# A fused FFN and mixer layer in two-part fp32: gate and up pieces moved in between the first modulation units, x's root from token rows, filler matmuls at the norms

## What is computed

```python
mod_ctx = (silu(c_ctx)[None] @ w_ada[l] + b_ada[l]).reshape(1, N_MOD, D_MODEL)
h = adaln_in(x, g[0], sh(0), sh(1))                 # rmsnorm(x, g) * (1 + scale) + shift
x = x + 0.5 * sh(2) * rmsnorm(swiglu(h, p['w_gate'][0], p['w_up'][0], p['w_down'][0]), g[1])
h = adaln_in(x, g[2], sh(3), sh(4))
mix, new_ml, new_ssm = hybrid_mixer(h, p, ml_state, ssm_state, n_seg)
x = x + sh(5) * rmsnorm(mix, g[3])
h = adaln_in(x, g[4], sh(6), sh(7))
x = x + 0.5 * sh(8) * rmsnorm(swiglu(h, p['w_gate'][1], p['w_up'][1], p['w_down'][1]), g[5])
```

## Time and profile before

| | |
|---|---|
| median of 3 runs | 3184.39 us (3184.34 to 3184.51) |
| the profiled execution: its own time, its span | 3184.13 us, 3182.3 us |
| granted clock of PE, mean over the span | 0.981 of 2.4 GHz |
| busy share PE / PEld / DVE / ACT / POOL | 96% / 91% / 42% / 31% / 57% |
| read from memory | 519 MB, 51% of the DMA engines' time |

### The profile page before, as it was taken

How to read it: one execution, slowest core, us unless ns; L and a number is a source line. 1 busy time by engine, 2 the same in 40 slices (tenths; PEclk the granted TensorE clock), 3 DMA queues, 4 the chain that set the end, 5 groups by cost and what they waited for, 6 DMA issues and landing times.

```text
span 3182.3 us, 48743 instructions
## 1 busy us (share of the span) xinstructions
PE 3067.9 (96%) x17651; PEld 2888.2 (91%) x17651; DVE 1350.7 (42%) x3013; ACT 973.4 (31%) x1206; POOL 1829.4 (57%) x903
## 2 busy tenths in 40 slices
PE   6799999999999999899999999899999999999998
PEld 2499999999999999689999999699999999999997
DVE  0336665665656655585754353413442211100114
ACT  2232222222232223533432333432222222222221
POOL 2366556655565555546775445565655666566663
PEclk8799999999999999899999999899999999999999
DMA  9967556656666555345444544145545654444442
GB/s 335 299 205 233 194 192 201 222 191 207 196 206 220 191 195 191 120 138 156 140 132 129 120 112 164 54 139 172 178 140 162 161 144 124 129 127 128 125 125 92
DMA packets 519202, 532.22 MB, mean 167 GB/s; under 512 B 29275, under 2 KB 493635, under 8 KB 518211
## 3 DMA queue, kind: packets, MB, share of 16 engines
q1 hardware_dynamic: 483136, 509.67, 51.0%
q10 hardware_dynamic: 35971, 21.27, 2.5%
HBM read 519.12 MB, written 9.66 MB: 166 GB/s over the span
## 4 chain that ended last, share of the span: by engine, by line
POOL 39%; issue 28%; PE 25%; DVE 4%; DMA 2%; ACT 2%; POOLq 1%; ACTq 0%; DVEq 0%
POOL w_lo L2272 36%; PE banks L699 7%; PE banks L701 7%; PE banks L700 7%; POOL hid_lo L2292 1%; PE banks L759 1%; DMA AM<-in_w_in_dram 1%; DMA w_raw<-in_w_ada_dram 1%; DVE HB L1989 1%; PE banks L725 1%; PE banks L1015 0%; PE banks L1100 0%; PE banks L1120 0%; ACT AM L1214 0%; DVE banks L1571 0%
## 5 line engine op out<-in xcount | busy, mean ns | idle before, releaser
L2272 POOL TENSOR_TENSOR w_lo<-w_raw,w_hi 128x1024 fp32r<-128x1024 f32 x668 | 1599.4, 2400 | 1088.6 <-ACT w_hi L1195 1088.0
L699 PE MATMUL banks<-xn_hi,w_hi 128*128 128x384 f32 x3936 | 1342.9, 341 | 29.4 <-DVE xn_lo L1588 18.4
L701 PE MATMUL banks<-xn_hi,w_lo 128*128 128x384 f32 x3936 | 1321.8, 336 | 0.0
L700 PE MATMUL banks<-xn_lo,w_hi 128*128 128x384 f32 x3936 | 1321.8, 336 | 0.0
L1195 ACT ACTIVATE w_hi<-w_raw 128x1024 fp32r<-128x1024 f32 x668 | 706.6, 1061 | 1531.1 <-PE banks L701 714.8
L699 PEld LDWEIGHTS banks<-xn_hi,w_hi 128*128 128x128 f32 x3936 | 743.9, 189 | 51.8 <-issue 37.6
L700 PEld LDWEIGHTS banks<-xn_lo,w_hi 128*128 128x128 f32 x3936 | 743.9, 189 | 3.9 <-issue 2.9
L701 PEld LDWEIGHTS banks<-xn_hi,w_lo 128*128 128x128 f32 x3936 | 743.4, 189 | 0.0
L1657 DVE SCALAR_TENSOR_TENSOR banks<-w_raw,cT,banks 128x256 f32<-128x256 f32 x1372 | 550.6, 484 | 0.3
L1735 DVE TENSOR_TENSOR AM<-AM,banks 128x384 f32<-128x384 f32 x88 | 44.8, 551 | 622.8 <-PE banks L701 622.8
L699 PE MATMUL banks<-hid_hi,w_hi 128*128 128x384 f32 x704 | 238.0, 338 | 3.1 <-POOL hid_lo L2292 3.1
(11 more groups left out here) (251 smaller groups left out, 1812.9 us busy)
## 6 DMA issues: line engine op xcount, KB each, us to landing
w_raw<-in_w_ada_dram SPq DMA_DIRECT2D x288, 512.0 KB, 5.2
w_raw<-in_ffn_w_gate_dram SPq DMA_DIRECT2D x176, 512.0 KB, 3.8
w_raw<-in_ffn_w_up_dram SPq DMA_DIRECT2D x176, 512.0 KB, 3.7
w_raw<-in_ffn_w_down_dram SPq DMA_DIRECT2D x176, 512.0 KB, 3.7
w_raw<-in_w_in_dram SPq DMA_DIRECT2D x104, 512.0 KB, 3.7
w_raw<-in_w_out_dram SPq DMA_DIRECT2D x32, 512.0 KB, 3.5
HB<-row_wait ACTq DMA_DIRECT2D x12, 512.0 KB, 4.7
x_wait<-xT ACTq DMA_DIRECT2D x1, 3072.0 KB, 9.6
```

The source lines that it names most:

```text
L699: pe.matmul(out, wh, hi, start=start, stop=False)
L700: pe.matmul(out, wh, lo, start=False, stop=False)
L701: return pe.matmul(out, w_lo[:, w, off:off + P], hi, start=False, stop=stop)
L2272: pool.tensor_tensor(w_lo[:, slot(p), :], w_raw[:, p % NR, :], w_hi[:, slot(p), :].bitcast(F32), ALU.subtract).then_inc(w_lo_ready, 1)
```

## The change

1. The start gets 9 main pieces: quarters 0, 1, 2 of g and u of the first 256 hidden columns and of g of the second 256. Each is loaded behind the four a pieces of its unit v (`START_LOAD`) and multiplied between the third and fourth a piece of unit v + 1 (`START_MAIN`). The second g is summed in banks 4 and 5 (`gate_bank`). `START_PAIRS` sets the units at which the normed pairs are made. The first part of FFN 1 keeps 7 main pieces with the same 20 a and 4 b pieces. The loop and all later orders stay.
2. x is loaded first, all 16 transposes follow piece by piece, and x's mean square comes from DVE on token rows (`x_root`): bn_stats, a root of 128 x 3, a diagonal spread by one matmul over bank 5 and copied to SBUF. The squares, POOL's adds and the 384-wide root and inverse of x go.
3. Columns of a unit are made after the second a piece of the next one where no main piece comes before.
4. y is zeroed during unit 14 (FFN 1), and by quarters within g of the second 256 columns (FFN 2); DVE waits for it after the first part.
5. At y1 and y2 PE makes 20, at x1 and x2 34 extra products of 128 x 128 ones into bank 1 (`stay_awake`). A root on one column before each FFN tail loads ACT's table early (`warm`).
6. The fourth main piece behind x1 and x2 is split after 12 of the 16 normed tiles.

```diff
-LEAD_BODY = 2 * "aaam" + 6 * "aam" + 2 * SPREAD_END
+LEAD_BODY = "aaaaaamaaaamaaaaaaaaaaam" + SPREAD_END
-        main = [(kind, 0, q) for q in range(U) for kind in "gu"] + main[-2 * U:]
+        main = [(kind, 0, q) for q in range(0 if n else U - 1, U) for kind in "gu"] + main[-2 * U if n else -U - 1:]
-START_PIECES = ada_units(ADA_FIRST)
+START_LOAD = {5: ("g", 0, 0), 6: ("u", 0, 0), 7: ("g", 1, 0), 8: ("g", 0, 1), 9: ("u", 0, 1), 10: ("g", 1, 1),
+              12: ("g", 0, 2), 13: ("u", 0, 2), 14: ("g", 1, 2)}
+START_MAIN = {(v + 1, 2): piece for v, piece in START_LOAD.items()}
+START_PAIRS = {4: 0, 5: 1, 6: 2, 8: 3, 10: 4, 12: 5, 14: 6}
+WAKE_Y, WAKE_X = 20, 34
+ROOT_TILE = 10
+        def gate_bank(n, part, s):
+            return 4 if n == 0 and part == "first" and s else 0
# SP
+                sp.dma_start(x_tok[:, 0, :], A["x_prompt"][0]).then_inc(x_loaded, 16)
+                sp.dma_start(x_tok[:, 1:3, :], A["x_sample"][0].rearrange("(c p) n -> p c n", p=P)).then_inc(x_loaded, 16)
+                for p, (kind, v, q) in enumerate(START_PIECES):
+                    if p == 3:
+                        sp.wait_ge(x_loaded, 32)
# PE
+                def stay_awake(n):
+                    for _ in range(n):
+                        pe.matmul(psum[1][:, 0:P], ones[:, :], ones[:, :], start=True, stop=True)
+                    if name in ("y1", "y2"):
+                        stay_awake(WAKE_Y)
-                        if first_tile(v, q, 4) == KT - 1:
-                            added_sum("x0")
+                        if (v, q) in START_MAIN:
+                            kind, s, part = START_MAIN[v, q]
+                            pe.wait_ge(xT_ready, KT)
+                            pe.wait_ge(x_rows, 1)
+                            unit_piece(START_AT[kind, s, part], part, 4 * s if kind == "g" else 2, fresh=0)
+                        if t == ROOT_TILE:
+                            pe.wait_ge(x_diag, 1)
+                            pe.matmul(ROOT_BANK[:, 0:TOK], ones[:, :], x_dia[:, :, :].rearrange("p c t -> p (c t)"), start=True, stop=True).then_inc(x_spread, 1)
...
+                stay_awake(WAKE_X)
# ACT
+                            if kind == "u" and early:
+                                for m in MAIN[N_START + 2:N_START + 2 + AHEAD]:
+                                    make_hi(m)
+                    act.activation(warm[:, :], eps[:, 0:1], ACT.Sqrt)
+                for t in range(KT):
+                    act.wait_ge(xt_tr, t + 1)
+                    act.activation(xT[:, t, :], psum[2 + t % 2][:, 0:TOK], ACT.Copy).then_inc(xT_ready, 1)
+                    if t == 3:
+                        act.wait_ge(x_ms, 1)
+                        act.activation(x_sqs[:, 1, :], x_sqs[:, 0, :], ACT.Sqrt, bias=eps[:, 0:1]).then_inc(x_std, 1)
-                hi_of(1)
+                hi_of(1, range(12))
+                make_hi(ahead(P_GATES))
+                hi_of(1, range(12, KT))
# DVE
-                    dve.wait_ge(y_zeroed, n + 1)
                     for part, it0, times in FFN_PARTS[n]:
                         if times == 1:
                             step(part, it0, None)
+                            dve.wait_ge(y_zeroed, n + 1)
+                def x_root():
+                    dve.wait_ge(x_loaded, 32)
+                    for c in range(NCH):
+                        for b in range(4):
+                            last = dve.bn_stats(x_stats[:, c, b, :], x_tok[:, c, 512 * b:512 * b + 512])
...
+                    if v == 1:
+                        x_root()
+                    if v == min(START_PAIRS):
+                        dve.wait_ge(x_spread, 1)
+                        dve.wait_ge(xT_ready, KT)
+                        dve.tensor_copy(x_root_rows, ROOT_BANK[:, 0:TOK]).then_inc(x_rows, 1)
# POOL
-                for k in range(KT):
-                    pool.wait_ge(sq_ready, k + 1)
...
+                for v in range(ADA_FIRST):
+                    if v in START_PAIRS:
+                        even_low(0, (2 * START_PAIRS[v],))
+                    if v in START_LOAD:
+                        make_lo(START_AT[START_LOAD[v]])
+                    if v == max(START_LOAD):
+                        pool.wait_ge(xt_tr, KT)
+                        pool.wait_ge(x_ms, 1)
+                        pool.memset(y[:, :, :], 0.0).then_inc(y_zeroed, 1)
...
+                            if n and part == "first" and (kind, s) == ("g", 1):
+                                last = pool.memset(y[:, 4 * q:4 * q + 4, :], 0.0)
-                even_low(2)
-                pool.memset(y[:, :, :], 0.0).then_inc(y_zeroed, 1)
+                even_low(2, range(0, 12, 2))
+                make_lo(ahead(FFN2))
+                even_low(2, range(12, KT, 2))
```

More of the change, by code:

```diff
@@ L161 @@
 N_PE = counts(lambda p: KINDS[p] != "b")
+for n, piece in enumerate(START_ORDER):
+    N_PE[START_AT[piece]] = n + 1
 N_B = counts(lambda p: KINDS[p] == "b")
@@ L601, in wait_evicted @@
                 eng.wait_ge(y_done, Y2_BASE + 2 * OUT_DONE.index(t) + 2)
+        FRESH_FIRST = [P_GATES, FFN2]
+        assert all(p in M_OF for p in FRESH_FIRST)
         with nc.Block() as block:
@@ L764, in added_sum @@
                     base, count = SQ[name]
-                    last = KT if name == "x0" else SUMMED
+                    last = SUMMED
                     pe.wait_ge(*SQ_USED[base + last - 1])
@@ L1183, in split @@
                 def split(p, i=None, per=0):
-                    p = ahead(p)
-                    if p is not None:
+                    first, p = p, ahead(p)
+                    if p is not None and first not in FRESH_FIRST:
                         make_hi(p, i, per)
@@ L1223, in ffn, with posts @@
                 def ffn(n):
-                    def posts(it, s, kind, p_end, i, per):
+                    def posts(part, it, s, kind, p_end, i, per):
                         for f in range(2):
@@ L1573, in scaled @@
                 def scaled(stage, k):
+                    root = ROOT_BANK[:, 0:TOK] if stage else x_root_rows
                     if k >= 4:
@@ L1745, in step @@
                             if kind == "a":
+                                if q == 1 and pending is not None:
+                                    ada_store(pending, i)
+                                    pending = None
                                 if q == U - 1:
@@ L2297, in step @@
                         for p, kind, s, q in pieces:
-                            if kind not in "ab":
+                            early = part == "first" and n == 0 and s == 0
+                            if kind not in "ab" and not early:
                                 split(p, i, per)
+                            if n and part == "first" and (kind, s) == ("g", 1):
+                                last = pool.memset(y[:, 4 * q:4 * q + 4, :], 0.0)
+                                if q == U - 1:
+                                    last.then_inc(y_zeroed, 1)
                             if kind == "u" and q == U - 1:
                                 hid_lo_part(it0, s, i)
+                            if kind == "u" and early:
+                                for m in MAIN[N_START + 2:N_START + 2 + AHEAD]:
+                                    make_lo(m)
                     for part, it0, times in FFN_PARTS[n]:
```

122 lines of the change are left out of this document (65 added, 57 removed).

## The result

The changed kernel takes 3154.01 us (median of 4 runs, 3152.16 to 3155.58) against 3184.36 (4 runs, 3183.98 to 3184.51): a ratio of 0.9905, 95% interval 0.9887 to 0.9922. I had said 3148 in a range of 3138 to 3162, faster. Sign and range held; of the forecast gain of 36.4 us some 30 came.

The account below looks back on a forecast made before the run. PE's products were taken to bound most of the span, the DMA the start, and PE gaps the two norms. Gains of 22.9 + 4.4 + 9.1 = 36.4 us from 3184.13 gave a forecast of 3148 us, range 3138 to 3162.

Parts of the forecast that it names:

- The start, 22.9: Up to the end of step 0: PE ends it at 187.0 us against 209.9, a gain of 22.9.
- landing formula: Loads in the start: piece n lands at (n + 6) x 1.50 + 8.1 us; the last awaited, 97, at 162.6.
- 8 slots are 12 us, so SP is not held: Ring in the start: a slot frees 4 to 6 us after landing, so loads never wait for PE's slots.
- I take the full clock: PE's nine main pieces in the start: 4.16 us each, not the 6.3 of a piece begun cold.
- The norm behind FFN 1, 4.4: Gain there: 0.3 from the early table load, 1.5 from quicker squares, 2.6 from a warm first main piece.
- The norm behind the mixer, 9.1: Gain there: 1.5 for squares, 2.6 for the cold piece, plus POOL's delayed low part; 9.1 us in full.
- The extra products at 0.23 us: At the norms: 0.23 us a product, so 34 take 7.8 us and 20 take 4.6, inside PE's gaps.
- Costs put at nothing: Start and loop: x first, x_root, the spread root and zeroing at unit 14 cost 0; the loop is identical.
- The half-cold start: Rival: the start's nine pieces run at 6.3 us, 12 to 14 us lost, 3161; chance 0.15.
- Extra products of no use: Rival at the norms: the clock falls anyway or they overrun by 1 to 3 us; 3156, chance 0.10.
- The DMA ending last: Rival: loads hold PE in step 0 and the loop's first step, the start's gain is gone; 3171, chance 0.04.
- PE at 1.2 GHz through the start: Rival: a unit takes 12.3 us against 7.5, 27 us lost in the start; slower at 3198, chance 0.04.

Follow-up runs that it names:

- h1_all: Changed kernel, step 0's first last-quarter g made two a pieces later, extra products there (3 each), before second g (11) and the tails (13, 14); 3147.59 us.
- g3_hold: Changed kernel with 24 extra products ahead of step 0's first last-quarter g piece and 11 ahead of the second g's; 3151.65 us, ratio 0.9901.
- e1_no_fillers: Changed kernel without the 20 and 34 extra products at the norms; 3157.85 us, ratio to before 0.9921, beside 3152.03 for the changed kernel.
- h3_changed: The changed kernel unaltered, run once more on another occasion; 3153.29 us, ratio to before 0.9906.
- g2_fill_9_11: Changed kernel with 9 extra products ahead of step 0's first last-quarter g piece and 11 ahead of the second g's; 3150.26 us, ratio 0.9897.

## Why the prediction was right, and where it was wrong

**Sign, range and mechanisms** held. The parts, each against the first two lines of the table:

**The start, 22.9, gave 17.7.** The sum was made of three numbers, and the landing formula itself was the sound one: it gave 137.1, 144.6 for the last quarters of g and u (137.43, 144.95 measured), and with the hold nearly gone, in h1_all, the second g piece came at 162.62. Two steps failed. First, "8 slots are 12 us, so SP is not held". A main piece in its place holds PE for the split (3.6) and for the product (4.2, here 6.7 as it ran slowly), and the a pieces behind it keep their slots as long; the DMA dipped to 207 GB/s and the second g piece landed 3.0 us late. By the nine traces at g3_hold, 1.1 to 1.6 us of this come with the product at full clock, the rest from its slow start. The prediction had compared one slot's time after landing with the length of the whole ring, though the landing itself takes its share of the 12 us; and it had checked this for the units of the start, not for step 0. Second, "I take the full clock". That was argued for the nine pieces inside the start, where it held for seven; but the sum then used it also for the five pieces behind a wait of 4.34 us, which took 23.1 us where 20.8 stood: 2.3 us. Together they make 5.3, and 5.2 are missing.

**The norm behind FFN 1, 4.4, gave 5.3.** The stretch to m1 gave 1.6 where 1.8 was said (0.3 for the table load and 1.5 for squares at full clock). The table load's price stood by the trace: the root now starts 0.03 us behind the end of PE's sums (1264.38 against 1264.35), before it was 0.34 (1282.49 against 1282.15), and e1_no_fillers has the gap behind them at 5.74 instead of 6.05. The squares' 1.3 came, but e1_no_fillers shows them nearly as quick without the extra products, so their cause is shown for 0.2 us only. Behind m1 it is 3.7 instead of 2.6. The excess of 1.1 lies where the change does nothing, and is luck as far as the traces tell. Products from 1400 to 1500 us, the kernel before and then the changed one:

```profile
1400.00:1500.00 100.00, 93.17 (x543) 92.11 (x543) 62.81 (x123) 38.00 (x49) 58.53 (x28) 0.95 0.46 133
```
```profile
1400.00:1500.00 100.00, 98.90 (x608) 97.22 (x607) 66.03 (x106) 37.59 (x43) 66.22 (x34) 1.00 0.53 155
```

The two windows don't hold quite the same work. Counted in steps of 20 us from m1, they do: the kernel before is under full clock at 0, 80, 100 and 160 us, the changed one at 80 only. The traces with 704.71 and 704.75 in the column to y2 are also low at 200 us (0.91), and the one with 706.60 at 100 and 200, where the same code elsewhere (703.1 to 703.3) is not.

**The norm behind the mixer, 9.1, gave 8.9**: 1.3 for the squares (1.5 said) and 7.6 for the cold piece, the wait on POOL and its cold stretch (7.6 said). It was the best term, as each of its parts had a row.

**The extra products at 0.23 us** came out at 0.23: 7.75 us for 34, 4.63 for 20. Between bounds of 0.21 and 0.64 the nearer rows had been the right choice. That those ahead of m1 and m2 keep the clock is shown by e1_no_fillers: 11 and 17 slow products without them, 0 and 1 with them.

**Costs put at nothing** were nothing: x first, x_root, the spread root and the zeroing at unit 14 left the landing at 137.43, 0.3 from the formula; the loop is equal to 0.01 us. (By that formula piece 8 lands at 29.1 us, where 28.5 stood; nothing hung on it.)

**The median.** I wrote that runs agree within 0.2 us, from three runs of the kernel before. That was luck: on the three chips of the experiments its own runs lie 2.7 to 3.2 us apart (3181.33 to 3184.55 over nine on one). Those of the changed kernel lie 3 to 5 us apart, and the profiled one was the quickest of four: 1.9 of the 6.0 us between 3148 and 3154.01 are this. By the table the difference between traces comes for the most part from counts of slow products that vary from execution to execution, and from landings in the start.

**The rivals.** The half-cold start did come in part: two of the nine pieces began slowly (5.7 and 6.0 us). It cost next to nothing, as the landing at 137.43 shows (0.3 from the formula), though the DMA was at 321 GB/s from 65 to 70 us; it cost where PE was the limit, in the last five. The Trainium skill (TensorE: Matmul & The Clock Gate, HAM oscillation) tells of a kernel in which each group of products, behind waits of some 3 to 5 us for the DMA, started cold. My prediction stretched this to all nine pieces, though it put a unit's gaps under 1 us itself. Seven of nine did not start slow here; the two that did stand behind a wait of 2.39 us that ended at 107.47, and behind thin work at a clock of 0.71 from 55 to 60 us. These are no test of the case that the page tells of; the waits of 9.17 and 9.26 us at the norms agree with it. Extra products of no use are excluded by e1_no_fillers. The DMA ending last, and PE at 1.2 GHz through the start, are excluded by the granted clock of 0.93 from 30 to 130 us and by the timeline.

## What to carry to other kernels

When matmuls are placed in a queue with loads that share one ring, ask what stands behind each one in order: the slots behind it are held for its split and its product, and a landing formula holds only while that is less than what the ring has left. Price a piece behind a wait like those here (2.2 to 9.3 us) at half clock for its first products: 5 to 19 of them were slow here, and once none. Or fill the wait: extra products sized to end when the operand is ready were worth 1.3 to 2.9 us at each tail and 0.2 to 2.6 in each of the four stretches at the norms, and they give it back when they run over.

## What the runs showed of the hardware

- Behind one and the same wait the number of slow products differs between executions of one program: 10, 20 and 21 behind the 3.14 us wait at the first tail (34.92, 36.24, 36.37 us to y1), over ten traces 2 to 21 (33.60 to 36.41 us). Two of each count are gaps between the first two pieces that the filled traces have too. With the wait filled, all three traces have 33.60 or 33.61. At the second tail, from its first product to the first of the last transposes, it is 32.74 or 32.75 filled and 34.08 to 35.61 not. The Trainium skill (TensorE: Matmul & The Clock Gate, Part 1) says that the point at which the clock rises depends on where in a free-running window the first matmul falls, and that it varies by 500 ns from run to run. The scatter here is wider: the products of the first tail stayed slow for 5.9 us in one trace (h3_changed), and none was slow in another (g3_hold). No run here can show the window.
- Extra products are themselves slow behind an idle stretch: 9 took 3.87 us (0.43 each) and 18 took 6.80 at step 0, against 0.23 each when PE had just been busy. The 11 ahead of the second g took 5.04 us in g2_fill_9_11, and 2.70 in h1_all, where the granted clock was 1.00 from 155 to 165 us. Their number has to be worked out from the idle time in us and from the clock that they will find, not from the price at full clock alone.
